# Convolution stage of a fused block: squares added on VectorE, another order of gates, splits and roots, and the second pair's rows ahead of a modulation chunk

## The chip, the cores and the metric

The kernel runs on one core of a Trainium2 chip. The metric is the device time of one execution in microseconds. A core has TensorE (PE, with its weight loads shown as PEld), VectorE (DVE), ScalarE (ACT), GpSimd (POOL, hardly used here) and SyncE (SP), which here issues all DMAs, in order, to one queue that 16 DMA engines serve.

## The reference, cut to what matters

Two blocks are computed one after the other on 256 tokens of width 1024, all in fp32. The first has two layers of a halved SwiGLU FFN, a mixer and another FFN; the mixer of layer 0 is the convolution module that this change is about:

```
def conv_module(h, w_pw1, w_dw, g_norm, w_pw2):      # h: rmsnorm(h, mix_norm), 256 x 1024
    a, b = split(h @ w_pw1)                          # 1024 x 2048
    u = a * sigmoid(b)
    u = causal depthwise convolution(u, w_dw)        # 31 taps, per channel
    u = silu(rmsnorm(u, g_norm))
    return u @ w_pw2                                 # 1024 x 1024
```

The second block takes the result as x, with a context of 256 tokens, modulation vectors from silu(c) @ w_mod + b_mod (w_mod: 1024 x 6144), a token mixer and 16 experts. The modulation products and the norm of the context depend on nothing of the first block, so the kernel does a part of them inside the convolution stage, where TensorE would have holes.

## The kernel before

**Data.** Activations lie with features on the partitions: `h` and others are [128, 8, 256] (8 tiles of 128 features, T = 256 tokens). Weights pass through `ring`, six slots of 1 MB. Slot n of the stream of loads is used again by load n + 6, so each load waits until its predecessor's slot is free (`wait_free`). The stream is: ffn0 (33), pw1 (8 slices of 256 columns), mod_conv (10: chunks 0 to 4 of w_mod, two slots each), pw2 (4 slices), mod_gap (2: chunk 5), ffn1, and so on. SyncE issues it in order.

**fp32 in three products.** For the FFNs, pw1 and pw2 each half of a slice is split by ScalarE into a high part (`split_hi`, L1626) and by VectorE into the rest (`split_lo`, L2165), in four buffers `w_split`. The second VectorE half frees the ring's slot. The activations are split likewise into `x_split`. `mm3` (L807 to L809) then multiplies high by high, high by low and low by high. A half takes 24 matmuls, a slice 48. `split_product` does one slice, first half, then second half. For the first slice (`first="pw1"` or `"pw2"`) the first half waits for x in four pieces of two feature tiles each.

**Norms.** ScalarE squares, TensorE sums over the partitions with a matrix of ones (`sum_squares`, eight matmuls, L840), ScalarE takes the root (`root`, L1614), VectorE the reciprocal (L2136). The FFN already adds its squares on VectorE to two tiles first (L2216, L2218) and needs two matmuls (L860).

**pw1 and gates.** Slices come in pairs (a, b) for four pairs of feature tiles. `glu_scale(pair)` scales both by the reciprocal root (L2308, L2313), ScalarE takes the sigmoid (L1742), `glu(pair)` multiplies (L2322) and marks the pair ready.

**Taps.** The 31 taps of pair 0 are done on VectorE: two tiles, 31 operations each (`taps`, L2347 and L2351), strewn between splits and gates by hand. Pairs 1, 2 and 3 are done on TensorE (`taps(pair)`, L986): SyncE stores the pair to DRAM (`keep_pair`, L678) and loads it again four times, shifted by one token each (`shift_pair`, L685; it waits until the stores have landed); VectorE spreads the tap weights into matrices (`spread_taps`, L2330). ScalarE copies the sums (`take_taps`, L1747) and squares them.

**Order of TensorE.** pw1; then `early_mod(0)` (a modulation product, `mod_product`, L967, from two slots, and `turn_mod`, L974, for the chunk before), `taps(1)`, `early_mod(1)`, `taps(2)`, `early_mod(2)`, the transposes of the context (L1010), `taps(3)`, `early_mod(3)`, sums for conv_out, `early_mod(4)`, sums for the context, four warming matmuls on zeros (L1021), and the four slices of pw2. The end of the stage is `conv_out`: root, reciprocal, eight scalings (L2145), Silu on ScalarE in four pieces (L1779, L1780), the low part on VectorE (L2157), pw2.

**Order of SyncE** in this stage: chunks 0 and 1, `keep_pair(1)`, `shift_pair(1)`, chunk 2, `keep_pair(2)`, `shift_pair(2)`, `keep_pair(3)`, `shift_pair(3)`, chunks 3 and 4, the four slices of pw2, chunk 5, ffn1.

## Time and profile before

| what | value |
|---|---|
| median of 3 runs | 1768.31 us (1767.81 to 1770.96) |
| profiled execution, its own time | 1771.32 us |
| its span on the core | 1769.5 us |
| TensorE busy | 1613.8 us, 91% |
| VectorE busy | 848.7 us, 48% |
| ScalarE busy | 678.9 us, 38% |
| DMA | 431.90 MB, mean 244 GB/s |

All durations below come from the one profiled execution; times are microseconds from the start of its span. The convolution stage reaches from about 205 (pw1 starts) to 327 (pw2 ends). The stages behind it are bound by TensorE up to about 1300 and by the loads of the experts' weights from there on.

### The profile page before, as it was taken

The numbers are of one execution on the slowest core, as the hardware profiler recorded it, in microseconds if no ns is written. First come the engines' busy times: TensorE is split into PE (matmuls) and PEld (weight loads), VectorE is DVE, ScalarE is ACT, GpSimd is POOL, SyncE is SP. The second block draws the span as 40 slices with busy tenths as digits, with TensorE's granted clock in tenths as the row PEclk, the third lists the DMA queues.
The fourth block names the chain that finished last, engine by engine and source line by source line (L and its number), as shares of the span: only waits on it lengthen the run. The fifth ranks groups of instructions, "written<-read, shape, count | busy, mean of one in ns | idle before, by whom it ended". The sixth has DMA issues, their size and how long they took to land.

```text
span 1769.5 us, 31746 instructions
## 1 busy us (share of the span) xinstructions
PE 1613.8 (91%) x13792; PEld 1375.0 (78%) x13799; DVE 848.7 (48%) x1159; ACT 678.9 (38%) x904; POOL 0.2 (0%) x4
## 2 busy tenths in 40 slices
PE   8999999999999999999999999999999866765765
PEld 7999986999999999879999979897885422422422
DVE  6556695855566555765655567965330000000001
ACT  5434544644454444554444456766311100100101
POOL 0000000000000000000000000000000000000000
PEclk9999999999999999999999999999999988888978
DMA  9755469655545655544655342346768999999997
GB/s 290 249 190 189 143 197 306 224 185 187 190 153 183 199 188 161 197 161 144 209 178 184 118 124 92 120 142 248 293 230 356 426 426 427 426 427 427 426 426 321
DMA packets 193903, 431.90 MB, mean 244 GB/s; under 512 B 8388, under 2 KB 150902, under 8 KB 178709
## 3 DMA queue, kind: packets, MB, share of 16 engines
q1 hardware_dynamic: 193812, 430.58, 67.2%
q8 instruction: 72, 1.18, 0.3%
q14 instruction: 19, 0.15, 0.0%
HBM read 428.62 MB, written 1.93 MB: 243 GB/s over the span
## 4 chain that ended last, share of the span: by engine, by line
PE 57%; DMA 22%; DVE 6%; ACT 2%; issue 1%; another core or an unknown queue 0%; DVEq 0%; SPq 0%; ACTq 0%
PE banks L807 11%; PE banks L809 11%; PE banks L808 11%; DMA arena<-in_w_exp_down 5%; DMA ring<-in_w_exp_gate 3%; DMA xn<-in_w_exp_up 3%; DMA squares<-in_w_exp_gate 3%; DMA h<-in_w_exp_down 3%; DMA arena<-in_w_exp_up 3%; DMA ring<-in_w_exp_up 2%; PE banks L1259 2%; PE banks L1261 2%; PE banks L1260 2%; PE banks L1404 2%; PE banks L1534 2%; PE banks L1438 1%
## 5 line engine op out<-in xcount | busy, mean ns | idle before, releaser
L2165 DVE TENSOR_TENSOR w_split<-ring,w_split 128x1024 fp32r<-128x1024 f32 x288 | 345.8, 1223 | 246.7 <-ACT w_split L1626 246.0
L807 PE MATMUL banks<-x_split,w_split 128*128 128x256 f32 x1600 | 453.3, 283 | 7.9 <-DVE w_split L2165 4.9
L809 PE MATMUL banks<-x_split,w_split 128*128 128x256 f32 x1600 | 448.9, 281 | 0.0
L808 PE MATMUL banks<-x_split,w_split 128*128 128x256 f32 x1600 | 448.9, 281 | 0.0
L1626 ACT ACTIVATE w_split<-ring 128x1024 fp32r<-128x1024 f32 x287 | 295.0, 1051 | 179.1 <-PE banks L809 171.7
L807 PEld LDWEIGHTS banks<-x_split,w_split 128*128 128x128 f32 x1600 | 302.5, 189 | 11.0 <-issue 5.6
L808 PEld LDWEIGHTS banks<-x_split,w_split 128*128 128x128 f32 x1600 | 301.8, 189 | 0.3
L809 PEld LDWEIGHTS banks<-x_split,w_split 128*128 128x128 f32 x1600 | 301.7, 189 | 0.0
L807 PE MATMUL banks<-hid_split,w_split 128*128 128x256 f32 x704 | 198.5, 282 | 0.5 <-DVE hid_split L2242 0.3
L809 PE MATMUL banks<-hid_split,w_split 128*128 128x256 f32 x704 | 198.0, 281 | 0.0
L808 PE MATMUL banks<-hid_split,w_split 128*128 128x256 f32 x704 | 197.5, 281 | 0.0
L2864 DVE TENSOR_TENSOR roots<-banks,roots 128x256 f32<-128x256 f32 x16 | 6.8, 425 | 267.0 <-PE banks L1534 267.0
L807 PEld LDWEIGHTS banks<-hid_split,w_split 128*128 128x128 f32 x704 | 132.9, 189 | 1.3 <-DVE hid_split L2242 1.3
L808 PEld LDWEIGHTS banks<-hid_split,w_split 128*128 128x128 f32 x704 | 132.4, 188 | 0.0
L809 PEld LDWEIGHTS banks<-hid_split,w_split 128*128 128x128 f32 x704 | 132.3, 188 | 0.0
L1534 PE MATMUL banks<-arena 128*32 128x256 f32 x992 | 73.2, 448 | 38.3 <-DMA arena<-in_w_exp_up 25.5
L1534 PEld LDWEIGHTS banks<-arena 128*32 128x32 f32 x992 | 34.5, 125 | 76.3 <-DMA arena<-in_w_exp_up 31.9
L1261 PE MATMUL banks<-x_hi,w_rest 128*128 128x256 f32 (+1 forms) x288 | 90.1, 313 | 0.0
L1685 ACT ACTIVATE hid_split<-gated 128x512 fp32r<-128x512 f32 x44 | 27.8, 632 | 148.5 <-DVE gated L2240 148.5
L2869 DVE TENSOR_TENSOR roots<-banks,arena 128x512 f32<-128x512 f32 x16 | 11.1, 692 | 141.2 <-PE banks L1540 141.2
L2227 DVE TENSOR_TENSOR gated<-banks,roots 128x512 f32<-128x512 f32 x88 | 60.4, 686 | 32.3 <-PE banks L809 32.2
L1259 PE MATMUL banks<-x_hi,w_gates 128*128 128x256 f32 (+1 forms) x216 | 70.5, 326 | 0.0
(484 smaller groups left out, 2289.2 us busy)
## 6 DMA issues: line engine op xcount, KB each, us to landing
ring<-in_ffn_w SPq DMA_DIRECT2D x131, 1024.0 KB, 5.3
arena<-in_w_exp_gate SPq DMA_DIRECT2D x13, 2048.0 KB, 45.5
ring<-in_w_mod SPq DMA_DIRECT2D x24, 1024.0 KB, 5.4
arena<-in_w_exp_down SPq DMA_DIRECT2D x12, 2048.0 KB, 45.1
arena<-in_w_exp_up SPq DMA_DIRECT2D x11, 2048.0 KB, 45.4
ring<-in_w_in SPq DMA_DIRECT2D x21, 1024.0 KB, 5.4
ring<-in_w_exp_down SPq DMA_DIRECT2D x9, 2048.0 KB, 44.3
ring<-in_w_exp_gate SPq DMA_DIRECT2D x7, 2048.0 KB, 46.1
```

Source lines behind the costliest of these rows:

```text
L807: mm(out_, hi, moving(0), start=start, stop=False, **kw)
L808: mm(out_, hi, moving(1), start=False, stop=False, **kw)
L809: return mm(out_, lo, moving(0), start=False, stop=stop, **kw)
L1259: mm(out_, hi, x_hi[:, k, rows], start=(k == 0), stop=False)
L1260: mm(out_, hi, x_rest[:, k, rows], start=False, stop=False)
L1261: last = mm(out_, lo, x_hi[:, k, rows], start=False, stop=(k == KD - 1))
L1404: last = mm(ps[:, 2 * j + o // 2, (o % 2) * T:(o % 2) * T + T], slot(n)[:, k * 512 + o * P:k * 512 + o * P + P], src[:, k, :], start=(k == ...
L1534: last = mm(ps[32 * q:32 * q + 32, 4 + m, 0:256], src(2 * j + k), w[:, k * D + 256 * q:k * D + 256 * q + 256], start=(j == 0 and k == 0), ...
L1626: fn(half_part(n, o, 0), half_slot(n, o, columns), ACT.Copy).then_inc(sem("half_hi"), 1)
L1685: fn(hid_split[:, c % 2, 0, :, :], hidden[:, c % 2, :, :], ACT.Copy).then_inc(sem("hid_hi"), 1)
L2165: ins = dve.tensor_tensor(half_part(n, o, 1), half_slot(n, o, columns), half_part(n, o, 0).bitcast(F32), ALU.subtract)
L2227: return dve.tensor_tensor(dst, ps[:, bank + c % 2, :].rearrange("p (k t) -> p k t", t=T), scale, ALU.mult)
```

## The change

- SyncE: `keep_pair(2)` goes ahead of chunk 2, and chunk 3 ahead of `shift_pair(3)`.
- The first slice of pw1 and of pw2 is done by a new `first_product`: each piece of x is multiplied with both halves of the slice as it comes. A matmul on zeros clears the bank first.
- The squares for conv_in, the context and conv_out are added on VectorE down to two tiles (`add_squares` and, for conv_out, additions pair by pair); `added_sums` then needs two matmuls in place of eight. The sums for conv_in stand between the halves of slice 1.
- ScalarE: the halves of pw1's slice 2 go ahead of the Silu of the modulation vectors; pair 0's squares go ahead of the context's copy; the halves of pw2's first slice go ahead of `take_taps(3)`; `root("conv_out")` goes ahead of `mod_copy(3)`; `mod_copy(4)` goes behind the four pieces of Silu.
- VectorE: the splits of pw1's slice 2 go ahead of the vectors' copies; `glu_scale(2)` and `glu(2)` come before further taps of pair 0, with the splits of slice 7 between them; the splits of pw2's first slice are taken apart, and the low parts of x are made between the scalings.
- TensorE: the four warming matmuls are gone; `turn_mod(2)`, chunk 4, `turn_mod(3)` and the context's sums come behind conv_out's sums.

```
@@ -37,3 +37,2 @@
 UKV_KEYS, UKV_VALUES, ROPE_BANK = 2, ((4, 0), (4, 7)), 5
-KEEP_WARM = 4
 BEGUN = 5
@@ -692,8 +691,8 @@
             shift_pair(1)
-            mod_chunk(2)
             keep_pair(2)
+            mod_chunk(2)
             shift_pair(2)
             keep_pair(3)
-            shift_pair(3)
             mod_chunk(3)
+            shift_pair(3)
             mod_chunk(4)
@@ -915,9 +914,9 @@
 
-            def split_product(n, bank, first=None):
+            def split_product(n, bank, between=None):
 
                 for o in range(2):
+                    if o == 1 and between is not None:
+                        between()
                     wait_split(n, o)
                     for k in range(KD):
-                        if first is not None and o == 0 and k % 2 == 0:
-                            wait_x(first, k // 2 + 1)
                         last = mm3(ps[:, bank, o * T:o * T + T], n, o, k, lambda part: x_split[:, part, k, :],
@@ -926,2 +925,25 @@
 
+            def first_product(n, bank, name):
+
+                if name == "pw1":
+                    pe.wait_ge(sem("h_updated"), 1)
+                mm(banks(bank, 1), zero_w[:, 0:P], zero_w[:, :], start=True, stop=False, skip_group_check=True)
+                for o in range(2):
+                    wait_split(n, o)
+                for k in range(KD):
+                    if k % 2 == 0:
+                        wait_x(name, k // 2 + 1)
+                    for o in range(2):
+                        last = mm3(ps[:, bank, o * T:o * T + T], n, o, k, lambda part: x_split[:, part, k, :],
+                                   start=False, stop=False, skip_group_check=True)
+                        if k == KD - 1:
+                            last.then_inc(half_done, 1)
+
+            def added_sums(count, bank, at=0):
+
+                pe.wait_ge(sem("conv_added"), count)
+                for k in range(2):
+                    last = mm(ps[:, bank, 0:T], ones[:, 0:P], squares[:, k, at:at + T], start=(k == 0), stop=(k == 1))
+                last.then_inc(sem("sumsq_ready"), 1)
+
             def square_product(name, n_slots, src, bank0=0, k_tiles=KD, half_cols=256, halves=None):
@@ -957,5 +979,6 @@
                     pe.wait_ge(sem("root_applied"), j // 2 - 1)
-                split_product(n, j % 4, first="pw1" if j == 0 else None)
                 if j == 0:
-                    sum_squares("conv_in", KD, T, 4)
+                    first_product(n, j % 4, "pw1")
+                else:
+                    split_product(n, j % 4, between=(lambda: added_sums(1, 4)) if j == 1 else None)
 
@@ -1013,12 +1036,16 @@
             taps(3)
-            early_mod(3)
-            pe.wait_ge(sem("squares_ready"), SQ_BEFORE["context"] + 1)
-            sum_squares("conv_out", KD, T, 7)
-            early_mod(4)
-            sum_squares("context", KD, T, 4, at=T)
-            pe.wait_ge(sem("mod_copied"), 5)
-            for _ in range(KEEP_WARM):
-                mm(banks(5, 1), zero_w[:, 0:P], zero_w[:, :], start=True, stop=True)
+            pe.wait_ge(sem("mod_copied"), 2)
+            mod_product(3, cond_pad, 6)
+            pe.wait_ge(sem("taps_copied"), 3)
+            added_sums(3, 7)
+            turn_mod(2, mod_rows, 4, T + 16)
+            pe.wait_ge(sem("mod_copied"), 3)
+            mod_product(4, cond_pad, 5)
+            turn_mod(3, mod_rows, 4, T + 24)
+            added_sums(2, 4, at=T)
             for j in range(4):
-                split_product(FIRST["pw2"] + j, j, first="pw2" if j == 0 else None)
+                if j == 0:
+                    first_product(FIRST["pw2"], 0, "pw2")
+                else:
+                    split_product(FIRST["pw2"] + j, j)
                 if j == 1:
@@ -1724,2 +1751,3 @@
             start_products(FIRST["pw1"], gains("mix_norm", 0), 1, "conv_in", 4)
+            split_hi_slot(FIRST["pw1"] + 2)
             act.wait_ge(sem("vectors_ready"), 1)
@@ -1727,3 +1755,2 @@
                ).then_inc(sem("cond_ready"), 1)
-            split_hi_slot(FIRST["pw1"] + 2)
             split_hi_slot(FIRST["pw1"] + 3)
@@ -1763,2 +1790,4 @@
             mod_copy(2, mod_rows, 5)
+            act.wait_ge(sem("conv_done"), 2)
+            square_pair(0)
             act.wait_ge(sem("pe_mark"), PE_MARK["ctx_turned"])
@@ -1767,10 +1796,7 @@
             fn(squares[:, :, T:2 * T], ctx_rows, ACT.Square).then_inc(sem("squares_ready"), 1)
-            act.wait_ge(sem("conv_done"), 2)
-            square_pair(0)
+            split_hi_slot(FIRST["pw2"])
             take_taps(3)
             square_pair(3)
-            split_hi_slot(FIRST["pw2"])
-            mod_copy(3, mod_rows, 6)
             root("conv_out", 7, D)
-            mod_copy(4, mod_rows, 5)
+            mod_copy(3, mod_rows, 6)
             for g in range(4):
@@ -1780,2 +1806,3 @@
                 fn(x_g, x_g, ACT.Silu).then_inc(sem("x_hi"), 1)
+            mod_copy(4, mod_rows, 5)
             root("context", 4, D, region=T)
@@ -2151,9 +2178,14 @@
 
-            def x_lo(name):
+            def x_lo(name, g):
 
-                for g in range(4):
-                    dve.wait_ge(sem("x_hi"), X_BEFORE[name] + g + 1)
-                    hi, lo = (x_split[:, part, 2 * g:2 * g + 2, :] for part in range(2))
-                    dve.tensor_tensor(lo, x_in[:, 2 * g:2 * g + 2, :], hi.bitcast(F32), ALU.subtract
-                                      ).then_inc(sem("x_split_ready"), 1)
+                dve.wait_ge(sem("x_hi"), X_BEFORE[name] + g + 1)
+                hi, lo = (x_split[:, part, 2 * g:2 * g + 2, :] for part in range(2))
+                dve.tensor_tensor(lo, x_in[:, 2 * g:2 * g + 2, :], hi.bitcast(F32), ALU.subtract
+                                  ).then_inc(sem("x_split_ready"), 1)
+
+            def add_squares(own):
+
+                step(dve.tensor_tensor(own[:, 0:4], own[:, 0:4], own[:, 4:8], ALU.add))
+                settle()
+                dve.tensor_tensor(own[:, 0:2], own[:, 0:2], own[:, 2:4], ALU.add).then_inc(sem("conv_added"), 1)
 
@@ -2287,4 +2319,8 @@
             dve.wait_ge(sem("h_updated"), 4 * 1)
-            split_lo_slot(FIRST["pw1"] + 1)
+            split_lo(FIRST["pw1"] + 1, 0)
+            dve.wait_ge(sem("squares_ready"), SQ_BEFORE["conv_in"] + 1)
+            add_squares(squares[:, :, 0:T])
+            split_lo(FIRST["pw1"] + 1, 1)
             root("conv_in")
+            split_lo_slot(FIRST["pw1"] + 2)
             dve.wait_ge(sem("pe_mark"), PE_MARK["rows_turned"])
@@ -2299,3 +2335,2 @@
             step(dve.memset(conv_in[:, :, PAD + T:PAD + T + 1], 0.0))
-            split_lo_slot(FIRST["pw1"] + 2)
             split_lo_slot(FIRST["pw1"] + 3)
@@ -2369,12 +2404,11 @@
             split_lo_slot(FIRST["pw1"] + 6)
-            taps((0, 6, 9), (1, 6, 9))
-            split_lo_slot(FIRST["pw1"] + 7)
-            spread_taps(4)
             glu_scale(2)
-            taps((0, 9, 11), (1, 9, 11))
+            split_lo(FIRST["pw1"] + 7, 0)
             glu(2)
+            split_lo(FIRST["pw1"] + 7, 1)
+            spread_taps(4)
             spread_taps(5)
-            taps((0, 11, 16), (1, 11, 16))
+            taps((0, 6, 10), (1, 6, 10))
             glu_scale(3)
-            taps((0, 16, 18), (1, 16, 18))
+            taps((0, 10, 11), (1, 10, 11))
             glu(3)
@@ -2382,7 +2416,26 @@
             spread_taps(7)
-            taps((0, 18, CONV_W), (1, 18, CONV_W))
-            split_lo_slot(FIRST["pw2"])
-            dve.wait_ge(sem("taps_copied"), 3)
-            normed("conv_out", x_in, conv_acc, gains("conv_norm"))
-            x_lo("pw2")
+            taps((0, 11, CONV_W), (1, 11, CONV_W))
+            before = SQ_BEFORE["conv_out"]
+            dve.wait_ge(sem("squares_ready"), before + 3)
+            step(dve.tensor_tensor(squares[:, 2:4, 0:T], squares[:, 2:4, 0:T], squares[:, 4:6, 0:T], ALU.add))
+            settle()
+            step(dve.tensor_tensor(squares[:, 0:2, 0:T], squares[:, 0:2, 0:T], squares[:, 2:4, 0:T], ALU.add))
+            settle()
+            dve.wait_ge(sem("squares_ready"), before + 4)
+            add_squares(squares[:, :, T:2 * T])
+            split_lo(FIRST["pw2"], 0)
+            dve.wait_ge(sem("squares_ready"), before + 5)
+            dve.tensor_tensor(squares[:, 0:2, 0:T], squares[:, 0:2, 0:T], squares[:, 6:8, 0:T], ALU.add
+                              ).then_inc(sem("conv_added"), 1)
+            root("conv_out")
+            for g in range(4):
+                for k in (2 * g, 2 * g + 1):
+                    ins = dve.scalar_tensor_tensor(x_in[:, k, :], conv_acc[:, k, :], gains("conv_norm")[:, k:k + 1],
+                                                   rstd[:, 0:T], ALU.mult, ALU.mult)
+                ins.then_inc(sem("piece_normed"), 1)
+                if g == 1:
+                    split_lo(FIRST["pw2"], 1)
+                if g > 0:
+                    x_lo("pw2", g - 1)
+            x_lo("pw2", 3)
             split_lo_slot(FIRST["pw2"] + 1)
```

## Rows read from the trace of the kernel before

**Rows 1.** The page, chain that ended last, by engine.
```profile
PE 57%; DMA 22%; DVE 6%; ACT 2%; issue 1%; another core or an unknown queue 0%; DVEq 0%; SPq 0%; ACTq 0%
```

**Rows 2.** Windows: PE, PEld, DVE, ACT, POOL busy, granted clock, DMA share, GB/s.
```profile
1450.00:1500.00 50.00, 32.00 (x323) 13.30 (x326) 3.06 (x8) 1.92 (x5) 0.00 (x0) 0.83 1.01 426
```

**Rows 3.** The chain of waits, convolution stage: start, duration, what.
```profile
244.57 0.36 PE banks L807
...
267.55 1.94 issue
...
278.52 15.93 DMA ring<-in_conv_w_pw
...
299.68 3.26 DVE xn L2145 x8
...
303.69 0.35 PE banks L807
...
315.17 0.79 PE banks L974 x8
...
335.88 0.99 PE banks L860 x4
```

**Rows 4.** Timeline of VectorE: start, duration, instruction, idle before and its releaser.
```profile
243.21 2.35 DVE L2165 TENSOR_TENSOR w_split<-ring,w_split 128x1024 fp32r<-128x1024 f32 x2
...
265.38 10.39 DVE L2351 SCALAR_TENSOR_TENSOR xn<-arena,w_dw_room,xn 128x256 f32<-128x256 f32 x26
295.62 2.36 DVE L2165 TENSOR_TENSOR w_split<-ring,w_split 128x1024 fp32r<-128x1024 f32 x2 [19.85 <-ACT w_split L1626]
...
333.74 1.22 DVE L2216 TENSOR_TENSOR squares<-squares 128x1024 f32<-128x1024 f32 x1
334.99 0.69 DVE L2218 TENSOR_TENSOR squares<-squares 128x512 f32<-128x512 f32 x1
```

**Rows 5.** Timeline of ScalarE.
```profile
216.05 0.48 ACT L1614 ACTIVATE roots<-banks,eps_col 128x256 f32<-128x256 f32 x1 [3.27 <-PE banks L840]
...
218.88 0.22 ACT L1726 ACTIVATE arena<-vec_b 128x16 f32<-128x16 f32 x1 [1.05 <-DVE w_dw_room L2293]
...
227.47 0.63 ACT L1742 ACTIVATE arena<-arena 128x512 f32<-128x512 f32 x1
...
294.54 2.00 ACT L1626 ACTIVATE w_split<-ring 128x1024 fp32r<-128x1024 f32 x2 [5.05 <-DMA ring<-in_conv_w_pw]
...
304.25 0.62 ACT L1780 ACTIVATE xn<-xn 128x512 f32<-128x512 f32 x1
...
306.56 4.13 ACT L1626 ACTIVATE w_split<-ring 128x1024 fp32r<-128x1024 f32 x4
```

**Rows 6.** Timeline of SyncE's DMA issues.
```profile
260.92 3.56 SPq L685 DMA_DIRECT2D arena<-kept  x4
...
270.36 2.53 SPq L685 DMA_DIRECT2D arena<-kept  x4
272.93 5.55 SPq L585 DMA_DIRECT2D ring<-in_w_mod  x4
```

**Rows 7.** Windows of the convolution stage, columns as in rows 2.
```profile
259.00:262.00 3.00, 3.00 (x63) 1.80 (x56) 3.00 (x8) 1.50 (x3) 0.00 (x0) 1.00 0.08 21
...
269.00:272.00 3.00, 2.51 (x48) 1.89 (x52) 3.00 (x9) 0.00 (x0) 0.00 (x0) 1.00 0.20 35
272.00:278.00 6.00, 6.00 (x104) 3.62 (x95) 3.78 (x10) 1.23 (x2) 0.00 (x0) 1.00 1.04 211
278.00:294.00 16.00, 16.00 (x195) 11.03 (x192) 0.00 (x0) 5.99 (x6) 0.00 (x0) 1.00 1.06 371
```

**Rows 8.** Timeline of TensorE near the start of the kernel.
```profile
11.89 0.55 PE L807 MATMUL banks<-x_split,w_split 128*128 128x256 f32 x1 [3.21 <-DVE w_split L2165]
```

**Rows 9.** Windows there, columns as in rows 2.
```profile
11.50:12.00 0.50, 0.11 (x1) 0.14 (x1) 0.50 (x2) 0.50 (x3) 0.00 (x0) 0.50 1.07 362
...
15.00:15.50 0.50, 0.50 (x6) 0.50 (x6) 0.50 (x2) 0.50 (x1) 0.00 (x0) 1.00 1.07 364
```

More of the change, by code:

```diff
@@ L692, in _ @@
             shift_pair(1)
+            keep_pair(2)
             mod_chunk(2)
-            keep_pair(2)
             shift_pair(2)
             keep_pair(3)
+            mod_chunk(3)
             shift_pair(3)
-            mod_chunk(3)
             mod_chunk(4)
@@ L1767, in _ @@
             fn(squares[:, :, T:2 * T], ctx_rows, ACT.Square).then_inc(sem("squares_ready"), 1)
-            act.wait_ge(sem("conv_done"), 2)
-            square_pair(0)
+            split_hi_slot(FIRST["pw2"])
             take_taps(3)
             square_pair(3)
-            split_hi_slot(FIRST["pw2"])
+            root("conv_out", 7, D)
             mod_copy(3, mod_rows, 6)
-            root("conv_out", 7, D)
-            mod_copy(4, mod_rows, 5)
             for g in range(4):
@@ L2369, in _ @@
             split_lo_slot(FIRST["pw1"] + 6)
[L2370 to L2371 removed]
+            glu_scale(2)
+            split_lo(FIRST["pw1"] + 7, 0)
+            glu(2)
+            split_lo(FIRST["pw1"] + 7, 1)
             spread_taps(4)
[L2373 to L2375 removed]
             spread_taps(5)
[L2377 removed]
+            taps((0, 6, 10), (1, 6, 10))
             glu_scale(3)
[L2379 removed]
+            taps((0, 10, 11), (1, 10, 11))
             glu(3)
```

2 lines of the change are left out of this document (removed).

## The prediction

> **What bounds the kernel now.** The page was read first, then the windows of the whole span, then the chain of waits between 244 and 316 us, and last the timelines of single engines there. The chain that ended last is 57% TensorE and 22% DMA [rows 1]. The DMA share belongs to the expert stage, where the engines of the queue are never idle (share 1.01, 426 GB/s) [rows 2]. Each load there waits for a buffer or for a mark that earlier work sets, so I let every microsecond won or lost in the convolution stage pass to the end one for one.
>
> In that stage the reader is to see where TensorE stands still. It computes the slices of pw1 until 256, then alternates tap sums and modulation products, waits 1.94 us at 267.55, and starts the first slice of pw2 at 303.69; 96 matmuls later, at 315.17, two slices are done [rows 3]. So a slice takes 5.74 us, and slice 1 starts at 309.43. The chain of waits says what holds slice 0: not the taps, but the load of pw2's first slice, 15.93 us from issue to landing at 294.4 [rows 3]. VectorE stands still for 19.85 us for it [rows 4], ScalarE for 5.05 us [rows 5], and the ScalarE halves stand ahead of the root there. The load is slow because it is queued: SyncE issues three shifts' loads and two modulation chunks just ahead of it [rows 6]. The DMA engines were almost empty at 259 to 262 and 269 to 272 (shares 0.08 and 0.20), then full from 272 on, at only 211 GB/s while the shifted rows come, at 371 GB/s behind them [rows 7].
>
> **Part 1, pw1.** Slice 0 of pw1 now takes each piece of x for both halves, so it no longer waits between pieces, and eight sums of squares give way to two. Two such sums are four records in 0.99 us [rows 3], so eight are near 3.7. TensorE reaches slice 1's second half about 4 us early. That does not last. The root (216.05 now, waiting for the sums) [rows 5] comes at 214.9, since it now stands behind slice 0, half of slice 1 and VectorE's two additions (1.22 and 0.69 us) [rows 4]. VectorE then puts two subtractions (2.3 us) ahead of the vectors, so the gate work on ScalarE starts at 220.05 and not 218.88, but of the four halves that follow it there only two (2.00 us a pair) still do [rows 5]: 220.05 - 218.88 - 1.95 = -0.78. The first sigmoid moves from 227.47 to 226.7. From there VectorE is the bound: it works without a break up to slice 6's halves at 243.21, for which TensorE waits at 244.57 already [rows 3, 4]. So slice 6 starts 0.77 us early, and of some 4 us on TensorE 3 turn into waits inside pw1. Behind it the order of gate and taps changes and their sum doesn't: the 26 last tap operations take 10.39 us now [rows 4], 0.395 each, and 40 of them take 15.8. The scaling of pair 3 now comes before slice 7 is done, 1.2 us of waiting, so the taps end at 276.2 (now 275.77). What hides this is the landing of the load; without that cover it would cost 0.4.
>
> **Part 2, the queue.** The second pair's gate comes at 247.7 in place of 254.7, since 10 tap operations and a spread no longer stand before it. Its four keeps are issued at 247.9 to 250.3, and chunk 2 behind them at 250.4 (now 247.8); its data has the shifted rows of pair 1 ahead of it until 252.5 anyway, so the move costs nothing. The shift of pair 2 is issued at 254 (now 260.92) [rows 6] and fills the first hole; the keeps of pair 3 at 258, chunk 3 at 260.6, the shift of pair 3 at 266.4 (now 270.36), chunk 4 at 269. The second hole is filled too. TensorE no longer waits 1.94 us before the taps of pair 2 and ends those of pair 3 at 285.9: 288.2 less 0.77 less 1.94, and a few tenths for shifted rows that land just in time. The first slice of pw2 can be issued only when chunk 2's first half is multiplied, near 275, and then has chunk 4 and the shift before it.
>
> When does it land? The queue moves the same bytes as before. By emptiness: the holes were worth (1 - 0.08) x 3 + (1 - 0.20) x 3 = 5.2 us [rows 7], a few tenths of ramp beside them, and all starts 0.77 earlier: 294.4 - 6.3 = 288.1. By bytes: from 271.9 on, 1.16 MB of shifted rows (128 partitions of 8 x 284 floats) at 211 GB/s, 4.2 MB of chunks and 1.05 MB of pw2 at 371 [rows 7] end at 291.6, 2.8 before the landing; laid end to end from 245.75, the new order gives 284.8, and with a lag of 0 to 2.8 the landing lies between 284.8 and 287.6. I take 287.7, since the lag shows at every load of the full stretch. The Trainium skill (DMA: Bandwidth & Descriptors, HWDGE ordering) says that a copy is split over many engines and that completion doesn't follow the order of issue; this would allow any landing between these ends, and the lag of 2.8 us agrees.
>
> **Part 3, from the landing to slice 1 of pw2.** Before, this took 309.43 - 294.4 = 15.0 us. Now the two halves on ScalarE stand ahead of the taps' copy and squares too: halves 2.02 [rows 5], copy and square 1.26 (0.63 each, as the sigmoid of the same 128x512) [rows 5], last addition 0.77 (0.69 and the hop) [rows 4], two sums 1.1 and hops 0.15 [rows 3], root 0.5, reciprocal 1.78, four scalings (0.41 apart) 1.6 [rows 3], the second half's subtraction 1.14. At landing + 10.3 the first low part starts, at + 11.05 slice 0. It takes all pieces for both halves and isn't held up by more than a tenth. Slice 1 doesn't follow at + 16.7: ScalarE does the four pieces until + 14.3, then copies chunk 4, loads a table, takes the context root and only then splits slice 1. From the last piece (304.25) to that split (306.56) it was 2.31 [rows 5], the copy adds 0.53, so + 16.55; 1.08 to VectorE, 1.29 to TensorE: **+ 18.9**. So the way from the landing grows by 3.9 us, while the landing comes 6.7 earlier. Slice 1 starts at 306.6, 2.8 us early. The sums for the context and chunk 4's product lie in the wait for x and cost nothing while they end by + 11: they end at + 10.05.
>
> **Part 4, the clock.** TensorE is done with chunk 3 at 287.8 and waits for the last addition until landing + 4.2 = 291.9: 4 us idle, and the four warming matmuls are gone. At the start of this trace a wait of 3.21 us [rows 8] was followed by a granted clock of 0.50 (1.2 GHz) at 11.5, which was 1.00 again at 15 [rows 9]. The two sums would then take 1.0 more on the path, and the products behind them use up the spare microsecond. I take 1.0; the bounds are 0 and 1.7 (a stretch of 3.4 us at half speed). The Trainium skill (TensorE: Matmul & The Clock Gate, Part 1: The HAM clock gate) calls half speed the state at rest, released by activity; the trace agrees (0.50 behind the 3.21 us), and this rule speaks against the change.
>
> **Sum.** 309.43 - (287.7 + 18.9 + 1.0) = 1.8 us. The profiled execution took 1771.32 (span 1769.5), so it would be 1769.5; the median of the runs lies 3.0 below the profiled one, so 1766.5. From 0.2% on, 3.5 us, a measurement of this kernel tells a change from none.
>
> **Rivals.**
> 1. The landing comes with little lag and the clock holds: landing 284.8 to 287, slice 1 at 303.7 to 305.9, won 3.5 to 5.7 us, 1762.6 to 1764.8. For it: chunk 4 alone stands ahead of the load, the clock was at 1.00 right behind the 1.94 us wait [rows 7]. Against it: the lag was never below 2 once the queue was full. It ends at 6.6 us, where the landing (283.9) stops being what ScalarE waits for and the taps of pair 3 take over. Chance 0.32.
> 2. The queue doesn't drain sooner, because the shifted rows (211 GB/s) and the keeps now travel among chunks and hold them up as much as the holes did. At a landing of 290.5 nothing is won, from 294.0 the change is slower by 3.5: the split of pw2's first slice stands ahead of the taps' copy now. At 294.4 the time is 1772.2. Against it: rows and chunks already travelled together at 272 to 278. Chance 0.05.
> 3. The clock stays at half through the slices, since light products and two waits follow. If slice 0 (5.7 us) alone runs at half it ends at 311, 1.7 us late and within the noise; if it lasts through slice 1 too, that slice ends at 322.5 and not 315.17: 1775. It decides from about 2 us into slice 1. For it: the removed warming matmuls. Against it: at 15 the clock was back after 3.5 us of products. Chance 0.06.
>
> The forecast has 0.57 (won 0 to 3.5 us, 1764.8 to 1768.3). Faster is rival 1, 0.32; slower are rivals 2 and 3, 0.11; the rest is within 0.2%. The range runs from rival 1's far end, 1762.6, to 1769.5, where two half-speed stretches or a landing at 290 would end.
>
> **What would show it.** In the profile after: no hole in the DMA share between 246 and 288; the first pw2 slice issued near 275 and landed near 287.7; no 1.94 us wait before the taps of pair 2; waits of TensorE inside pw1 (about 3 us together, before slices 2 and 6), whose end moves by less than 1 us; a wait of some 4 us before the two sums for the convolution, with a granted clock of 0.5 behind it; and ScalarE's root, table and split between slices 0 and 1 of pw2, for which TensorE waits 2 us. It is wrong if the load lands before 285 or after 290, if pw1 ends more than 2 us earlier, or if a wait further down changes size.

## The result, and the profile after

| | time before | time after | ratio |
|---|---|---|---|
| 20 runs each | 1769.79 us (1767.81 to 1773.76) | 1773.40 us (1769.82 to 1777.74) | 1.0015, 95% interval 1.0008 to 1.0022 |
| e1, 11 runs of after | 1770.88 us | 1772.16 us | 1.0009, 1.0000 to 1.0018 |

The ratios of this document are the record's estimates with their intervals; they lie near the quotient of the two medians but are not it (1.0020 for the 20 runs, where the estimate says 1.0015). The forecast was 1766.5, at most 1769.5, and faster; measured is slower by 0.15%. That is below the 0.2% from which the prediction would call a change, but the interval excludes 1. The profiled execution of the changed kernel took 1769.82 (span 1767.7) and is the fastest of its 20, that of before took 1771.32, 1.5 above its median. So the pair of profiles alone shows a gain that the runs do not have. Three profiles of each were read: spans 1769.5, 1768.3 and 1769.1 before, 1767.7, 1771.5 (e1) and 1769.3 (e15) after. "Landing" is below the moment when ScalarE starts to split pw2's first slice, since that is when the load is in. "Half clock" is a granted clock of 0.50 (1.2 GHz) where 1.00 is full (2.4 GHz).

A part of the loss lies outside the span. In every execution of before whose span is on record, and of the kernels made from it (e3, e7, e11), time less span is 1.7 to 1.9 us; in every execution of the changed kernel it is 2.1 to 2.2 us, as in those made from it (2.0 to 2.1 where pw1's old sums stand, e6 and e12). So some 0.4 us of the median's loss are not in the convolution stage. No run shows where they come from.

The chain of waits of the changed kernel, first profile, from the load to slice 1 of pw2, answers to [rows 3]; columns are start, duration, what:

```profile
274.84 14.47 DMA ring<-in_conv_w_pw
289.40 2.00 ACT w_split L1653 x2
291.40 0.49 ACT xn L1774
291.92 0.64 ACT squares L1629
292.58 0.70 DVE squares L2428
293.42 1.10 PE banks L946 x4
294.52 1.10 PE banks L997 x8
295.62 3.22 PE banks L990 x16
298.93 1.22 DVE w_split L2197
300.15 0.60 DVE x_split L2183
...
305.93 0.47 ACT roots L1641
306.40 0.96 ACT w_split L1653
307.38 1.24 DVE w_split L2197
308.66 0.39 PE banks L806
```

The load of pw2's first slice still heads the chain. It is issued at 274.84 and lands at 289.3. The order behind it is the predicted one up to the sums (L946). Then comes a step that the prediction did not have: chunk 4's product (L990, 16 matmuls, 3.22 us), and only behind it the low part of the slice's second half (L2197). Slice 1 starts at 308.66, 0.77 before the old 309.43.

TensorE's waits in the stage, from its timeline of the same profile (pw1's two, then the three behind it):

```profile
218.61 0.38 PE L806 MATMUL banks<-x_split,w_split 128*128 128x256 f32 x1 [0.87 <-DVE w_split L2197]
243.92 0.36 PE L806 MATMUL banks<-x_split,w_split 128*128 128x256 f32 x1 [2.18 <-DVE w_split L2197]
281.27 5.27 PE L1009 MATMUL banks<-arena 128*32 128x256 f32 x64 [2.84 <-DMA arena<-kept]
293.42 1.10 PE L946 MATMUL banks<-squares,consts 128*128 128x256 f32 x4 [1.71 <-DVE squares L2428]
308.66 0.39 PE L806 MATMUL banks<-x_split,w_split 128*128 128x256 f32 x1 [1.84 <-DVE w_split L2197]
```

The first two are the waits inside pw1 that were forecast, and so is the last, of some 2 us before slice 1, whose split stands behind a root on ScalarE. The third is for the shifted rows of pair 3: 2.84 us, where "a few tenths" stood. Its 64 tap matmuls then take 5.27 us, at half clock for the most part.

The same rows of the third profile (e15), the lower half of the stage:

```profile
281.92 3.66 PE L1009 MATMUL banks<-arena 128*32 128x256 f32 x64 [2.18 <-DMA arena<-kept]
294.10 1.32 PE L946 MATMUL banks<-squares,consts 128*128 128x256 f32 x4 [3.35 <-DVE squares L2428]
```

Here the same 64 matmuls take 3.66, the clock held, so TensorE reaches the sums sooner and waits for them longer, 3.35.

The windows over the waits and the products behind them; columns are TensorE's busy time, its granted clock, DMA share and GB/s. First profile of the changed kernel:

```profile
292.00:294.00 2.00, 0.58 (x3) 1.00 0.85 291
294.00:296.00 2.00, 2.00 (x15) 0.71 1.08 362
296.00:298.00 2.00, 2.00 (x12) 0.50 1.11 357
298.00:300.00 2.00, 2.00 (x18) 0.94 0.70 174
```

Second profile (e1):

```profile
292.00:294.00 2.00, 0.00 (x0) 0.85 1.08 374
294.00:296.00 2.00, 1.45 (x4) 0.50 1.10 357
...
304.00:306.00 2.00, 2.00 (x6) 0.50 0.93 297
306.00:308.00 2.00, 2.00 (x15) 0.73 1.02 371
```

Third profile (e15):

```profile
294.00:296.00 2.00, 1.90 (x9) 0.71 1.10 359
...
302.00:304.00 2.00, 2.00 (x7) 0.50 1.03 330
304.00:306.00 2.00, 2.00 (x13) 0.73 0.98 354
```

Half clock stands there for 3.4, 13.7 and 10.2 us. Each end is worked out from its window's mean: 0.71 over 2 us is 0.84 at full and 1.16 at half. All three profiles of before show 1.00 in every one of these windows. The numbers that decide, each from the timelines:

| profile | TensorE's waits before pair 3's taps and before the sums | pw2's first slice landed (its split starts) | half clock in or behind the sums' wait | end of slice 1 (its last matmul) | span |
|---|---|---|---|---|---|
| before, e13, e14 | none; none | 294.5, 294.8, 294.0 | none | 315.2, 315.5, 314.6 | 1769.5, 1768.3, 1769.1 |
| after | 2.84; 1.71 | 289.4 | 3.4 | 314.5 | 1767.7 |
| e1 | 1.06; 4.06 | 290.5 | 13.7 | 317.7 | 1771.5 |
| e15 | 2.18; 3.35 | 290.1 | 10.2 | 316.2 | 1769.3 |

The span less the end of slice 1 is 1452.8 to 1454.5 in all six: what these spans win or lose, they win or lose up to there. The mean end moved from 315.1 to 316.1. The landing came 4.4 us sooner (294.4 to 290.0), and the way behind it grew by 5.4.

### The profile page after: what moved, and what is told of

It reads as the page before. It is cut to its first block, busy times and chain, and to the rows that moved or that the text cites. A ratio compares the mean times of both kernels' runs of the same rounds, so it can differ in the third digit from the quotient of the medians.

```text
span 1767.7 us, 31684 instructions
## 1 busy us (share of the span) xinstructions
PE 1610.7 (91%) x13761; PEld 1367.5 (77%) x13761; DVE 854.4 (48%) x1166; ACT 678.3 (38%) x904; POOL 0.2 (0%) x4
## 4 chain that ended last, share of the span: by engine, by line
PE 56%; DMA 22%; DVE 6%; ACT 2%; issue 1%; another core or an unknown queue 0%; DVEq 0%; ACTq 0%
PE banks L806 11%; PE banks L808 10%; PE banks L807 10%; DMA arena<-in_w_exp_down 5%; DMA ring<-in_w_exp_gate 3%; DMA xn<-in_w_exp_up 3%; DMA h<-in_w_exp_down 3%; DMA squares<-in_w_exp_gate 3%; DMA arena<-in_w_exp_up 3%; DMA ring<-in_w_exp_down 2%; PE banks L1286 2%; PE banks L1288 2%; PE banks L1287 2%; PE banks L1431 2%; PE banks L1465 1%; PE banks L1561 1%
## 5 line engine op out<-in xcount | busy, mean ns | idle before, releaser
L2197 DVE TENSOR_TENSOR w_split<-ring,w_split 128x1024 fp32r<-128x1024 f32 x288 | 345.9, 1223 | 232.5 <-ACT w_split L1653 231.8
```

The source lines that it names most:

```text
L2197: ins = dve.tensor_tensor(half_part(n, o, 1), half_slot(n, o, columns), half_part(n, o, 0).bitcast(F32), ALU.subtract)
```

## The experiments

They are told in groups. A ratio is to before on the same chip, with its 95% interval. A profile is one execution, and not always a typical one; where it lies far from its kernel's median, the text says so.

**The two kernels again.** e1, e15 are the changed kernel, e13 and e14 the one before.

> The changed kernel once more, to see whether its convolution stage is the same in every execution. Theory A (the load of pw2's first slice lands sooner, the way behind it is longer, and the granted clock falls in the waits of TensorE before the taps of pair 3 and before the sums; where it falls differs from run to run): slice 1 of pw2 starts between 308.5 and 311.5, with half clock in other places than 281 to 285 and 295 to 299; the median lies 1 to 4 us above the kernel before. Theory B (the queue: shifted rows and slice land later in most executions than in the one profiled): the first pw2 slice lands at 291 or later (289.3 in the profile after) and slice 1 starts at 310 or later with little change of the clock. Theory C (nothing in the stage; the time is lost in the experts' stage): slice 1 starts at 308.7 within 0.5, and the execution is longer behind 1320.

> The kernel before once more, for a second profile of it; nothing is left out. Theory A says that the half clock behind TensorE's waits befalls both kernels: then this profile shows half clock in at least one place of the convolution stage (the likeliest is behind the wait ahead of the taps of pair 2), and the second matrix's slice 1 ends 1 to 3.5 us later than the 315.0 us of the first profile. If half clock is the changed kernel's alone, the granted clock stays at 1.00 from 205 to 330 us and the slice ends at 315.0 us within 0.7.

> The kernel before a third time, with the same two outcomes: half clock in at least one place of the convolution stage and the second matrix's slice 1 ending 1 to 3.5 us behind 315.0 us if the fall befalls both kernels, 1.00 throughout and 315.0 us within 0.7 if it is the changed kernel's alone. Two profiles that agree say more than one.

> The changed kernel once more, for a third profile of it; nothing is left out. Theory A: the second matrix's first slice lands between 289 and 291.7 us, the clock is at half in two places or more of the convolution stage, and slice 1 ends between 314.3 and 319 us, with the span 1453 to 1455.5 us behind that end. If the time is lost in the experts' stage instead, the span is more than 1456 us behind it.

Measured: the table above; e1's median of 1772.16 is 1.3 us above before's, as its theory A said, and slice 1 started near 311.9, where 308.5 to 311.5 was said. Three profiles of three of the changed kernel have half clock in the stage, and none of three of before. So theory A of e13 and e14, that it befalls both, found nothing. It is not excluded for every execution: kernels made from before show half clock too, behind waits of 2.08 us (e7, in pw1), 2.09 us (e11) and 5.01 us (e3), and e11's wait is the one that before has (1.94). Theory A's numbers for e15 came (landing 290.1, half clock in two places, 316.2, span 1453.1 behind), and theory C, a loss in the experts' stage, has no support in these profiles: the remainder is constant.

**The queue: old order, and new order alone.** e2 puts SyncE's old order into the changed kernel; e3 is the opposite, only the new order in the kernel before.

```
             shift_pair(1)
+            mod_chunk(2)
             keep_pair(2)
-            mod_chunk(2)
             shift_pair(2)
             keep_pair(3)
-            mod_chunk(3)
             shift_pair(3)
+            mod_chunk(3)
             mod_chunk(4)
```

> The changed kernel with the old order of SyncE alone: chunk 2 ahead of the stores of pair 2, the shifted rows of pair 3 ahead of chunk 3. Theory A: the holes of the queue come back, the first pw2 slice lands near 293 to 294, slice 1 starts at 312 to 313, 3 to 4 us later than in the changed kernel. Theory B: shifted rows come no later than now and the time falls by 1 to 3 us. Theory C: no change of more than 1 us in the total.

> The kernel before with the new order of SyncE alone. Its gate of pair 2 is ready at 254.7 only, so chunk 2 would wait for the stores there. Theory A: one hole of the queue is filled at best, the landing moves by less than 2 us, the time by less than 2 us either way. Theory B: slower by 1 to 3 us, since chunks now hold up the shifted rows. Theory C: no change.

Measured: e2 1776.34, ratio 1.0029 (1.0019 to 1.0040); e3 1776.23, 1.0029 (1.0018 to 1.0040), where e3's theory A said less than 2 us either way. The new order is worth having only with the new order of gates. In e3 `keep_pair(2)` waits for the late gate and chunk 2 waits behind it: the DMA share at 254 to 258 is 0.18, TensorE waits 5.01 us before the taps of pair 2. In e2 the holes are back (0.62 at 258 to 270), the slice lands at 293.5, TensorE waits 7.83 us before the sums, and slice 1 ends at 321.9. So Part 2 was a gain inside this change, and the loss had to be elsewhere.

**One transfer each.** e17 puts `shift_pair(3)` back ahead of chunk 3, e18 moves only the load of pw2's first slice ahead of chunk 4, e10 does both.

```
             keep_pair(3)
+            shift_pair(3)              # e17, e10
             mod_chunk(3)
-            shift_pair(3)              # e17, e10
+            cols(FIRST["pw2"], conv_w_pw2[0], 0, 256, KD)   # e18, e10
             mod_chunk(4)
-            for j in range(4):
+            for j in range(1, 4):      # e18, e10
```

> The changed kernel with that queue order alone. Theory A: landing at 281 to 286, sums at 288 to 290, slice 1 starts at 303 to 305 behind ScalarE's root and split (a wait of 1.8 us stays), 3 to 5 us below the changed kernel, 1 to 4 below the kernel before; half clock in pw1 in some executions. Rival: chunk 3 or 4 lands too late, less than 2 us are won.

> The changed kernel with the shift of pair 3 back ahead of chunk 3, and nothing else moved; nothing is left out. Theory A: the wait of 2.2 to 2.8 us before the taps of pair 3 goes, so the half clock behind it goes too, the first slice of pw2 still lands at 288.5 to 291.5 us, and the total is 1.5 to 3 us below the changed kernel (ratio to before 0.9998 to 1.0008). If the move of the shift costs nothing, the total stays that of the changed kernel, 1.0012 to 1.0018 of before.

> The changed kernel with the load of pw2's first slice ahead of chunk 4, and nothing else moved; nothing is left out. Theory A: the first slice lands near 285 us, 4 us sooner, the wait before the taps of pair 3 stays at 2 to 3 us and holds the convolution's sums to 291 us or later, and the total lies between the changed kernel and the slice-first run: ratio to before 0.9988 to 1.0003. If the landing alone sets the end, the ratio is that of the slice-first run, 0.997 to 0.999.

Measured: e10 1766.22, ratio 0.9981 (0.9972 to 0.9990); e17 1774.78, 1.0026 (1.0016 to 1.0036); e18 1767.66, 0.9984 (0.9975 to 0.9993). e10 met its marks: the slice landed at 285.0, slice 1 started at 303.7. e17 refutes what I had made of the wait for the shifted rows. TensorE's waits there, before the sums and before slice 1, from its timeline, and four windows:

```profile
294.83 2.04 PE L946 MATMUL banks<-squares,consts 128*128 128x256 f32 x4 [5.91 <-DVE squares L2428]
311.81 0.39 PE L806 MATMUL banks<-x_split,w_split 128*128 128x256 f32 x1 [1.83 <-DVE w_split L2197]
```

```profile
292.00:294.00 2.00, 0.00 (x0) 0.50 1.10 349
300.00:302.00 2.00, 2.00 (x13) 0.50 0.36 31
...
312.00:314.00 2.00, 2.00 (x12) 0.60 0.05 4
314.00:316.00 2.00, 2.00 (x12) 0.54 0.89 258
```

The wait for the rows is gone, the landing is not sooner (290.8), and so the whole 5.9 us stand in one wait before the sums, where they had been two (2.18 + 3.35 in e15). The clock is at half from 291.9 to 302.1, the first 2.9 us of it inside the wait. Slice 1 ends at 319.2, 28.4 us behind the landing, where e15 took 26.1. But this half clock is no longer than e15's (10.2 us in both), and less of it falls on work. Most of the 2.3 us come later: behind the wait of 1.83 us before slice 1 the clock is at half once more, for 3.4 us, and slice 1 takes 7.4 us, where it takes 5.8 in the first profile of the changed kernel and in e4. So this pair of profiles does not show that one long wait costs more than two short ones, and the intervals of e17 and of the changed kernel overlap. What e17 shows is that the wait for the rows is not what costs the time.

The same second stretch of half clock, inside slice 1 and behind a wait of 1.8 us, stands in the profiles of e2, e5, e6, e10 and e18 (slice 1 takes 7.4 to 7.5 us in each). Of the eight profiles with this wait only two, the first of the changed kernel and e4's, have full clock behind it.

e18 keeps the wait for the rows (1.84 us) and still wins: the slice lands at 285.1, TensorE waits 0.48 us before the sums:

```profile
282.32 3.66 PE L1010 MATMUL banks<-arena 128*32 128x256 f32 x64 [1.84 <-DMA arena<-kept]
291.63 1.10 PE L947 MATMUL banks<-squares,consts 128*128 128x256 f32 x4 [0.48 <-DVE squares L2429]
298.63 0.36 PE L807 MATMUL banks<-x_split,w_split 128*128 128x256 f32 x1 [1.08 <-DVE x_split L2184]
306.38 0.39 PE L807 MATMUL banks<-x_split,w_split 128*128 128x256 f32 x1 [1.81 <-DVE w_split L2198]
```

This order is faster than both kernels, and its only edit is the place of one load. The profile itself is e18's slowest execution (1771.90, 4.2 above its median): slice 1 ends at 313.7, of that 1.6 us by half clock inside it, and the rest of the span is 1456.0, 1.5 or more longer than in the table.

e11 moves the same load in the kernel before.

> The kernel before with one line of the queue moved: the first slice of pw2 ahead of chunk 4. Theory A: the slice lands near 289 in place of 294.4, the root for the convolution no longer stands behind the splits and comes at 294.5 in place of 296.9, slice 0 starts 2 to 2.4 us earlier, the total is 1.5 to 2.5 us below the kernel before. Rival: the load wasn't what set slice 0, but the sums on TensorE or chunk 4's product: less than 0.7 us.

Measured: 1771.08, 1.0002 (0.9992 to 1.0013), where 1.5 to 2.5 us of gain were forecast. The profile is one of the slower executions (1773.84). ScalarE no longer waits for the load, but there the last taps, a sum of eight matmuls and chunk 4 hold it: slice 0 starts at 307.1 with a half clock of 7 us behind TensorE's wait of 2.09 us before the taps of pair 2. By the medians, the move gains only together with the changed kernel's other orders.

**The clock.** e4 fills the waits before the taps of pair 3 and before the sums with products on zeros, e5 also those inside pw1. In both the wait for chunk 2's copy (`mod_copied`) stands ahead of the first zero products.

```
+            for _ in range(11):
+                mm(banks(5, 1), zero_w[:, 0:P], zero_w[:, :], start=True, stop=True)
             taps(3)
...
+            for _ in range(7):
+                mm(banks(5, 1), zero_w[:, 0:P], zero_w[:, :], start=True, stop=True)
             added_sums(3, 7)
```

> The changed kernel with 11 matmuls on zeros (2.4 us) ahead of the taps of pair 3 and 7 (1.5 us) ahead of the convolution's sums, both in the waits of TensorE that the profile shows (2.84 and 1.71 us). Theory A: the granted clock stays at 1.00 through the stage, chunk 4's product takes 1.9 in place of 3.2 us, the second half of pw2's first slice isn't held up, slice 1 starts 0.5 to 2 us earlier and the median falls by 1 to 3 us. Theories B and C: the clock may stay up, but the total moves by less than 0.7 us.

> The warming matmuls of e4, and matmuls on zeros in the waits inside pw1 too: 3 ahead of slice 2 and 9 ahead of slice 6. In e1 and e4 the granted clock fell at 245 behind the wait of 2.2 us ahead of slice 6 and pw1 ended at 257.6 and 257.3 in place of 255.4. Theory A (waits of TensorE bring the clock down, in pw1 as before the sums): no half clock from 205 to 330, pw1 ends at 255.2 to 255.8, slice 1 of pw2 starts at 305.5 to 308, and the time is 1 to 3 us below e4's against the same kernel before, so 0.5 to 3 us faster than before. Theory A' (the fall in pw1 has another cause than the wait): half clock near 245 again. Theory C (the experts' stage): the total stays where e4 was.

Measured: e4 1771.53, 1.0002 (0.9993 to 1.0011); e5 1771.42, 1.0001 (0.9992 to 1.0010). In e4's profile the clock is 1.00 from 250 on, so from before the taps of pair 2, the slice lands at 289.0 and slice 1 ends at 313.6, so the way behind the landing is 24.6 us. I take this as the undisturbed length: with it, the three profiles of the changed kernel lose 0.5, 2.5 and 1.5 to the clock, 1.5 on average. e5's profile has full clock in pw1, where the zero products stand, and ends pw1 sooner than e4, as its theory A said. But it is not at full clock throughout, as theory A wanted: behind the wait before slice 1, which neither e4 nor e5 fills, it is at half for 3.4 us (0.82, 0.50 and 0.82 in the windows from 308 to 314). In the times e4 and e5 stand at before's level, not 1 to 3 us better; against e1 of the same chip e4 wins 0.6 us, less than the intervals resolve. So the clock's cost is seen in profiles and not in the medians, and no run fills the wait before slice 1 too.

**pw1.** e6 takes the old first slice and eight sums of squares into the changed kernel, e7 the new ones into the kernel before.

```
                 if j == 0:
-                    first_product(n, j % 4, "pw1")
...
+                    sum_squares("conv_in", KD, T, 4)
...
-            add_squares(squares[:, :, 0:T])
```

> The changed kernel with pw1's old first slice and its eight sums for conv_in behind slice 0 (two halves one after the other, no additions on VectorE there). Theory A: TensorE has 4 us more work in pw1 and waits less than 1 us ahead of slice 6, so the clock stays at 1.00 in pw1 in every execution; pw1 ends at 256 to 257; the total is 0 to 2 us better than the changed kernel's. Rival (the saving on TensorE counts): pw1 ends 2 to 4 us later than in the profile after (255.4) and the total is worse by as much.

> The kernel before with the front part of the change alone: first slice of pw1 by pieces, two sums for conv_in between the halves of slice 1, slice 2's splits ahead of the vectors. Theory A: waits of some 1 and 2 us inside pw1, pw1 ends 0.7 us earlier at full clock and 1 to 1.5 us later where the clock falls; pw2's first slice lands when it did, so the total is -1 to +1 us. Rival (the saving on TensorE counts): pw1 ends 2 us or more earlier and the total falls by 1 us or more.

Measured: e6 1774.38, 1.0016 (1.0007 to 1.0025); e7 1771.11, 1.0000 (0.9991 to 1.0009). e7 shows the front part worth nothing in the kernel before, as Part 1 had it. In e6 the wait in front of slice 6 is 0.74 us and pw1 is at full clock, yet the median is 2.2 us above e1's on the same chip and not 0 to 2 better; the intervals of the two overlap, so in the changed kernel a small gain by the front part is neither shown nor excluded.

**The splits behind the landing.** e8, e9 and e12 take the two ScalarE halves of pw2's slice 1 apart, one ahead of the Silu pieces and one ahead of chunk 4's copy; e8 also calculates chunk 4 ahead of the sums, e9 and e12 have e10's queue. e16 is e10 with both halves right behind the Silu pieces. e8, e9 and e16 have zero products in pw1's waits, e8 also before the taps of pair 3; e12 has the old pw1 and none.

```
-            mod_copy(4, mod_rows, 5)
-            root("context", 4, D, region=T)
-            split_hi_slot(FIRST["pw2"] + 1)
+            split_hi_slot(FIRST["pw2"] + 1)
+            mod_copy(4, mod_rows, 5)
+            root("context", 4, D, region=T)
```

> e5 with three more moves: chunk 4's product ahead of conv_out's sums (it fills the wait there in place of zeros, and pw2's second half no longer waits for its slot), the first half of pw2's slice 1 split on ScalarE ahead of the Silu pieces, the second half ahead of the copy of chunk 4 and the context's root. Theory A: slice 0 of pw2 starts at 299.5 to 301, slice 1 follows it without the wait of 1.8 us, at 305 to 307; the total is 1.5 to 3 us below e5's and 3 to 6 us below the kernel before. If the path runs elsewhere, slice 1 doesn't move.

> The changed kernel with the first slice of pw2 loaded ahead of chunk 4, the shifted rows of pair 3 ahead of chunk 3 as before, the early splits of e8 for slice 1 of pw2, and matmuls on zeros in the two waits inside pw1. Theory A (the stage is bound by the landing of the first pw2 slice, 289 to 291.7 in the changed kernel's profiles, and by the way behind it): the slice lands at 281 to 286, TensorE has no wait before the taps of pair 3, the sums for the convolution come at 288 to 290 (293.4 to 295.7 so far), slice 1 starts at 301 to 303.5, the clock stays up, and the total is 5 to 8 us below the kernel before. Rival (another load, chunk 3 or 4, now lands too late for its product and takes the place): slice 1 starts at 306 or later and the total is within 3 us of the kernel before.

> e9 with pw1's old first slice and eight sums for conv_in (as in e6), without any matmuls on zeros. Theory A: no wait above 1 us in pw1 and so no half clock there; pw1 ends at 256.7; everything behind is 0.5 to 1.5 us later than in e9; the total is 4 to 7 us below the kernel before. If the front part of the change is worth its 3 us on TensorE, e12 is 2 us or more behind e9.

> The changed kernel with the queue of the slice-first run (shifted rows ahead of chunk 3, the second matrix's first slice ahead of chunk 4), zero products of TensorE in the two waits inside pw1, and both halves of the second matrix's slice 1 split on VectorE right behind the four Silu pieces' work, ahead of chunk 4's copy and of the context root. Nothing is left out. Theory A (landing, and the splits behind it, hold slice 0 and slice 1): slice 0 starts at 294 to 296.5 us, slice 1 ends at 306 to 309 us, and the total is 1 to 3 us below the slice-first run's, 4 to 7 below before. Rival: another wait takes the place of the one removed, and the total is the slice-first run's within 1 us.

Measured: e8 1769.48, 0.9992 (0.9983 to 1.0001); e9 1768.24, 0.9992 (0.9982 to 1.0001); e12 1769.66, 0.9996 (0.9987 to 1.0005); e16 1766.06, 0.9975 (0.9966 to 0.9984). e8, e9 and e12 missed their marks: 3 to 6, 5 to 8 and 4 to 7 us below before were forecast, and the ratios say 1.4, 1.4 and 0.7. In all four the wait of 1.8 us before slice 1 is gone. A half ahead of the Silu pieces doesn't pay as far as the medians go (e9 is behind e10 by 2.0 us, with intervals that overlap): in e9 and e12 ScalarE itself then waits 2.3 us for the load of slice 1. e16 met its marks (slice 0 at 296.2, slice 1's end 307.7, 3.4 before e10's, of which 1.6 are e10's half clock in slice 1), but not its time, 0.2 below e10's median, not 1 to 3: the rival held. In the profiles the lead is still 2.4 us at 1280; then the windows of the router, e16 and e10 in this order, show where some 2 us of it go:

```profile
1312.00:1328.00 16.00, 14.63 (x118) 0.79 0.53 193
```

```profile
1312.00:1328.00 16.00, 13.98 (x132) 1.00 0.65 248
```

Whether this half clock befalls e16 in most executions is open. The three profiles of before have 0.89 in this window; e1 and e15 have 1.00 there and 0.89 in the next 16 us.

## Why the prediction was wrong

**What held.** Part 1: the root came at 215.0 (214.9 said), the first sigmoid at 226.8 (226.7), slice 6 at 243.9 behind a wait of 2.2 us, pw1's end at 255.4. Part 3: landing to slice 1's start, +18.9, was 19.3 in the first profile, and without half clock (e4) landing to the end of slice 1 was 24.6, where 18.9 + 5.74 makes 24.6.

**Part 2, the landing: the step that failed first.** The holes were filled: the mean share from 246 to 282 was 1.07, 1.06 and 1.07 in the three profiles (0.85 before), and still the landing was 289.4 to 290.5, mean 290.0, and not 287.7. The 2.3 us are the largest term that the profiles show. The prediction added a lag of 0 to 2.8 to the 284.8 of its byte count; measured from there it is 4.6 to 5.7. A likely reason, worked out and not tested by a run that takes the successor away, is that a load shares the engines with the one behind it: slice 1's load is issued 0.86 us behind (275.70). The queue runs dry just when slice 0 lands, here by the windows at 286 to 294 of the first profile (width, clock, DMA share, GB/s):

```profile
286.00:290.00 4.00, 1.00 0.84 273
290.00:294.00 4.00, 1.00 0.46 159
```

1.05 MB at 350 GB/s are 3.0 us; by 289.3 almost all of both was in. First in, first out would have had slice 0 near 286.3, already 1.5 behind the 284.8 of the sum. In e1 and e15 the landing is later by another 1.1 and 0.7. There the wait of 2.1 to 2.2 us inside pw1, which the sum priced at nothing, brought the clock to half for 3.4 us, pw1 ended later, and the load was issued at 277.0 and 276.2, not 274.8. That alone isn't the reason: in e4 all of this is the same (issued at 276.8), and the slice landed at 289.0. The rest is open. The Trainium skill (DMA: Bandwidth & Descriptors, HWDGE ordering) says that completion does not follow the order of issue. It gives no size for it.

**Part 4, the clock: mis-sized.** It counted one light stretch, 1.0 us, with 1.7 (3.4 us at half) as its bound, and rival 3, that it stays at half, had 0.06. Measured in and behind the sums' wait: 3.4, 13.7 and 10.2 us at half, cost of all half clock behind the landing 0.5, 2.5 and 1.5. The bound came from a start of the trace where products of 128x256 stood behind the wait [rows 8, 9]; here the 40 matmuls behind it are light, and the clock came back only within the slice (e1, e15) or among the 40 (first profile). The work on the path then doubles, in the chain of the second profile:

```profile
294.55 2.05 PE banks L946 x4
296.60 1.50 PE banks L997 x8
298.10 3.57 PE banks L990 x16
301.67 1.80 PE banks L997 x8
303.47 1.92 PE banks L946 x4
```

Chunk 4's product takes 3.57 here and 1.92 at full clock, and with it comes the wait that Part 3 left out: the low part of the slice's second half (L2197) counts slots in order and so waits for chunk 4 to free its own. VectorE's timeline of the third profile has it:

```profile
300.62 1.23 DVE L2197 TENSOR_TENSOR w_split<-ring,w_split 128x1024 fp32r<-128x1024 f32 x1 [1.21 <-PE banks L990]
301.77 0.68 DVE L2183 TENSOR_TENSOR x_split<-xn,x_split 128x512 fp32r<-128x512 f32 x1
```

It is 0.41 us in the first profile, nothing in e4, 1.21 in e15. "They end at + 10.05", the cover that made the light products cost nothing, held only at full clock: in e1 they end at 305.38, 14.9 behind the landing. The Trainium skill (TensorE: Matmul & The Clock Gate, Part 1: The HAM clock gate) calls half speed the state at rest. The runs agree (0.50 within the waits of 4.06 and 5.91 us), and say besides that the wait of 2.1 to 2.2 us before slice 6 is followed by either level: by 1.00 in the first profile and e2, by 0.50 in e1 and e15. The prediction priced no half clock behind that wait, nor behind the wait of 2 us before slice 1; the second costs 1.6 us where it comes (e17 and five more), though in none of the changed kernel's three: the first keeps full clock there, and in e1 and e15 slice 0 is so late that slice 1 follows without a wait.

**The sum, again.** Predicted end of slice 1: 287.7 + 18.9 + 1.0 + 5.7 = 313.3. Measured mean: 290.0 + 24.6 + 1.5 = 316.1. The difference is 2.3 of landing and 0.5 of clock; it turns the forecast gain of 1.8 into a loss of 1.0. The forecast's rival 2 says that nothing is won at a landing of 290.5. It leaves out the 1.0 for the clock; with it, 289.5 is that point, and all but one of the landings lie behind it. A third error lies in the baseline: 3.0 us from profile to median came from three runs; over 20 it is 1.5, and this alone puts the forecast 1.5 too low.

**Open.** The three profiles say 1.0 us slower at the end of slice 1, and 0.4 come outside the span. The ratios 1.0009 and 1.0015 say 1.6 and 2.7, the medians 1.3 and 3.6. So between nothing and some 2 us of the loss are in no profile. The changed kernel's three profiled executions took 1769.82, 1773.65 and 1771.52, on average 1771.7, below both its medians (1773.40 and, in e1, 1772.16), so they may be the milder ones. The half clock inside slice 1 (1.6 us), which six of eight profiles with that wait have, could fill a part of the gap, but no profile of the changed kernel shows it. How the loss divides between landing and clock in the times isn't resolved either; e4 and e1 differ by 0.6. What is shown is that the landing decides the sign: with it at 285, e10 and e18 are faster than before.

## What to carry to other kernels

When a wait is removed, ask where its idle time goes. Moving one transfer ahead (e17) turned waits of 2 and 3 us into one of 6 and won nothing. List every wait of TensorE of 2 us or so, and price the half clock behind each, by what follows it and not by the wait alone. Put the load that heads the chain ahead of the bulk that is needed later, and allow for its landing later than the bytes ahead of it say: here 4.6 to 5.7 us later, with the next load queued behind it. And one profile is one execution: where the clock falls in some and not in others, take three of each kernel before explaining a difference of 2 us.

## What was not expected of the hardware

The same wait of 2.1 to 2.2 us between the same dense products of pw1 was followed by a granted clock of 1.00 in one profile of the changed kernel and by 0.50 in two. Over all nine profiles with this wait it is 1.00 in two (the first and e2) and 0.50 in seven. The window behind it, first in the profile after, then in e15:

```profile
244.00:246.00 2.00, 2.00 (x17) 1.00 0.08 9
```

```profile
244.00:246.00 2.00, 2.00 (x10) 0.50 0.18 16
```

And the two waits of pw1 and slice 1, short ones between dense products, brought half clock more often than not, each time for 3.4 us (from the windows of e1, e5 and e17).
